# Twelve weight blocks of the second layer's gate moved from TensorE in layer 0 to VectorE in layer 1

## The reference, cut to what matters

```
for l in range(2):
    mod = silu(c) @ w_ada[l] + b_ada[l]              # 2048 -> 6144, one vector
    shift, scale, gate = split(mod, 3)               # 2048 each
    h = rms_norm(x, norm_g[l]) * (1 + scale) + shift
    u, z_s, q, k, v, z_a = split(h @ w_in[l])        # 2048 -> 6144
    y_s = s5_mixer(u, ..., w_glu[l]) * silu(z_s)     # a scan, then 1024 -> 2048
    y_a = diff_attention(q, k, v) * silu(z_a)
    y = concat([y_s, y_a]) @ w_out[l]                # 2048 -> 2048
    x = x + gate * y
```

## Time and profile before

| | us |
|---|---|
| three runs | 2893.7, 2898.98, 2899.66 |
| their median | 2898.98 |
| the profiled execution | 2895.5 |
| its span in the trace | 2893.6 |
| TensorE busy, VectorE busy | 2781.8, 2008.9 |
| layer 0's `w_outa`, `w_glu`, `w_outm` | about 524 to 693 |
| layer 1's `w_outa`, `w_glu`, `w_outm` | 1045.7 to 1185.0 |

### The profile page before, as it was taken

The page is one execution under the profiler, slowest core; times in us unless marked ns, Lnnn a source line. Parts: engine busy times, 40 slices in busy tenths (PEclk is TensorE's granted clock), DMA queues, the critical chain, the costliest instruction groups (busy, mean ns, idle before and its releaser), DMA issues.

```text
span 2893.6 us, 64415 instructions
## 1 busy us (share of the span) xinstructions
PE 2781.8 (96%) x27664; PEld 2593.9 (90%) x27664; DVE 2008.9 (69%) x3478; ACT 1468.2 (51%) x2406; POOL 288.5 (10%) x488
## 2 busy tenths in 40 slices
PE   6899999999999999999999999999999999999987
PEld 2678788788999999999889889999999999999987
DVE  6357778687799986765556566666888547887565
ACT  3335556355566656644444435456555445555454
POOL 0012222100123221200011011100000000000000
PEclk9899999999999999999999999999999999999999
DMA  9988788885756566555444445554555555555543
GB/s 392 332 267 269 260 287 267 292 310 169 205 171 199 175 204 197 181 175 169 140 144 150 140 133 170 180 193 161 185 182 187 184 184 180 181 185 187 182 153 110
DMA packets 168236, 581.08 MB, mean 201 GB/s; under 512 B 40272, under 2 KB 40304, under 8 KB 155536
## 3 DMA queue, kind: packets, MB, share of 16 engines
q1 hardware_dynamic: 146784, 525.40, 54.2%
q0 software_dynamic: 20592, 48.26, 5.4%
q10 hardware_dynamic: 576, 3.31, 0.3%
HBM read 555.06 MB, written 21.76 MB: 199 GB/s over the span
## 4 chain that ended last, share of the span: by engine, by line
PE 84%; DVE 7%; DMA 6%; ACT 1%; issue 1%; SPq 1%; POOL 0%; DVEq 0%; ACTq 0%
PE acc L1011 82%; DMA arena<-in_w_ada 3%; DVE arena L979 2%; PE acc L1014 2%; DVE rounded L979 2%; DMA scr_k<-arena 1%; DMA arena<-scr_k 1%; SPq L976 1%; DVE upper L987 1%; DMA scr_u<-upper 0%; DVE arena L987 0%; ACT arena L1008 0%; DVE rounded L987 0%; DVE upper L979 0%; DMA arena<-in_w_outm 0%
## 5 line engine op out<-in xcount | busy, mean ns | idle before, releaser
L1011 PE MATMUL acc<-rounded 128*128 128x256 f32 x14592 | 1861.9, 286 | 18.6 <-issue 10.1
L1011 PEld LDWEIGHTS acc<-rounded 128*128 128x128 f32 x14592 | 1783.5, 192 | 86.2 <-issue 61.2
L1008 ACT ACTIVATE rounded<-arena 128x1024 fp32r<-128x1024 f32 (+1 forms) x862 | 875.3, 1022 | 694.5 <-PE acc L1011 583.5
L979 DVE TENSOR_TENSOR rounded<-arena,rounded 128x1024 fp32r<-128x1024 f32 (+1 forms) x830 | 983.9, 1198 | 246.7 <-ACT rounded L1008 246.1
L1011 PEld LDWEIGHTS acc<-upper_rounded,rounded 128*128 128x128 f32 x4656 | 560.8, 192 | 18.2 <-issue 9.8
L1011 PE MATMUL acc<-upper_rounded,rounded 128*128 128x256 f32 x4656 | 567.7, 284 | 2.8 <-DVE rounded L979 2.0
L1008 ACT ACTIVATE arena<-arena 128x256 f32<-128x256 f32 (+3 forms) x473 | 232.9, 515 | 170.8 <-DVE arena L979 105.4
L979 DVE TENSOR_TENSOR arena<-acc,arena 128x256 f32<-128x256 f32 (+5 forms) x270 | 113.7, 431 | 233.7 <-PE acc L1011 221.0
L979 DVE TENSOR_TENSOR arena<-arena 128x256 f32<-128x256 f32 (+5 forms) x455 | 233.3, 526 | 35.9 <-ACT arena L1008 27.5
L987 DVE SCALAR_TENSOR_TENSOR arena<-arena 128x256 f32<-128x256 f32 (+5 forms) x465 | 205.1, 446 | 27.7 <-ACT arena L1008 19.6
L1011 PE MATMUL acc<-arena 128*32 128x512 f32 (+6 forms) x1990 | 183.2, 402 | 41.7 <-DMA arena<-in_w_ada 27.6
(11 more groups left out here) (92 smaller groups left out, 1116.0 us busy)
## 6 DMA issues: line engine op xcount, KB each, us to landing
arena<-in_w_in SPq DMA_DIRECT2D x328, 512.0 KB, 4.8
arena<-in_w_ada SPq DMA_DIRECT2D x88, 1024.0 KB, 5.5
arena<-in_w_up SPq DMA_DIRECT2D x176, 512.0 KB, 3.9
arena<-in_w_down SPq DMA_DIRECT2D x88, 512.0 KB, 4.2
arena<-in_w_outa SPq DMA_DIRECT2D x32, 512.0 KB, 6.0
arena<-in_w_glu SPq DMA_DIRECT2D x32, 512.0 KB, 5.8
arena<-in_w_outm SPq DMA_DIRECT2D x32, 512.0 KB, 4.6
arena<-in_w_out SPq DMA_DIRECT2D x32, 512.0 KB, 3.8
```

Of the source, the lines that this page charges most:

```text
L979: return self.put(self.e and self.e.tensor_tensor(o, a, b, op))
L1008: return self.put(self.e and self.e.activation(o, a, f, scale=scale, **kw))
L1011: return self.put(self.e and self.e.matmul(o, l, r, start=start, stop=stop, skip_group_check=True))
```

## The change

- The units of columns 9, 10 and 11 of layer 1 (12 MB of w_ada, the gate of rows 4 to 15) are taken out of layer 0's background. `later` has columns 8 to 11 of layer 0 in one group of four and columns 0 to 8 of layer 1 in groups of three.
- A new generator `g_modv` runs in layer 1 from `w_outa` on. GpSimd loads each unit (`modv_load`, 128x2048, two buffers); the first two loads wait for the scan's last y, each later one for the unit two before it. VectorE multiplies each of a unit's four 128x512 blocks by one value per partition and adds it up (`modv`: one TENSOR_SCALAR for the first block of a column, else SCALAR_TENSOR_TENSOR). At a column's end TensorE sums over the partitions by four matmuls with one column of ones (`modv_end`), and VectorE adds the bias.
- Layer 1's `w_outa` tiles ("xb") are now copied by ScalarE from PSUM into free places of SBUF (`late_tile`). `late_x(n)` adds tile n to x once its gate is known: tiles 0 to 3 after `w_outa`'s tile 3, the others after `modv_end`. An xf tile waits for its late_x.

```diff
 MOD_REST = (2, 3, 2)
+MODV = (9, 10, 11)
+MODV_REST = (6, 1, 1)
...
+        if t.kind == "xb":
+            if n == 7:
+                act.wait_ge("s5_act", ("y", 1, 15))
+            act.act(V(late_tile(n), 256), pv, ACT.Copy).then_inc("ev_act", key)
...
-        later = then(self.modulation(0, range(8, 12), (7,), 2), self.modulation(1, range(12), (7,), 3))
+        later = then(self.modulation(0, range(8, 12), (7,), 4), self.modulation(1, range(MODV[0]), (7,), 3))
+
+        def g_modv():
+            while ("s5", 1, 15) not in self.marks:
+                yield
+            for _ in range(2):
+                yield
+            for u in range(2):
+                self.add("modv_load", u)
+            while ("w_outa", 1, 3) not in self.marks:
+                yield
+            for n in range(4):
+                self.add("late_x", n)
+            for u in range(4 * len(MODV)):
+                for i in range(4):
+                    self.add("modv", u, i)
+                    for _ in range(self.modv_rest):
+                        yield
+                if u + 2 < 4 * len(MODV):
+                    self.add("modv_load", u + 2)
+                if u % 4 == 3:
+                    yield
+                    self.add("modv_end", u // 4)
+                    for n in range(4):
+                        self.add("late_x", 4 * MODV[u // 4] - 32 + n)
+                        yield
...
+    def modv_end(j):
+        pe.wait_ge("modv_dve", (4 * j + 3, 3))
...
+        for i in range(4):
+            x = pe.mm(B(5, i, 1), V(MACC + 512 * (j % 2) + 128 * i, 128), con("ones", 1), True, True)
+        x.then_inc("mod_pe", ("col", (1, MODV[j])))
...
+    def modv(u, i):
+        dve.wait_ge(f"l_mv{u % 2}", u)
...
+            x = dve.ts(acc, w, c, None, MUL)
+        else:
+            dve.wait_ge("modv_dve", (u, i - 1) if i else (u - 1, 3))
+            x = dve.stt(acc, w, c, acc, MUL, ADD)
...
+    def late_x(n):
+        x = V(X + 256 * n, 256)
+        dve.wait_ge("ev_act", ("ev", tl.out_of["w_outa", 1, n].o))
+        dve.wait_ge("mod_dve", ("mod", (1, 8 + n // 4)))
+        dve.stt(x, V(late_tile(n), 256), V(MODC + 80 + n, 1), x, MUL, ADD).then_inc("late_dve", n)
...
+                if t.kind == "xf":
+                    dve.wait_ge("late_dve", n)
...
+    def modv_load(u):
+        if u < 2:
+            pool.wait_ge("s5_act", ("y", 1, 15))
+        else:
+            pool.wait_ge("modv_dve", (u - 2, 3))
+        pool.dma(V(MWS[u % 2], 2048), D["w_ada"][48 + 4 * MODV[0] + u], f"l_mv{u % 2}", u)
```

More of the change, by code:

```diff
@@ L90, in const_array @@
     put("c8", np.broadcast_to(np.arange(32) * 8, (128, 32)))
-    put("quad", p[:, None] % 32 == np.arange(3)[None, :])
+    put("quad", p[:, None] % 32 == np.arange(4)[None, :])
     put("nsgn", np.where(top, -1, 1))
@@ L182, with late_tile @@
 SQF = N1 + 5632 + 6 * 256
+def late_tile(n):
+    return (PQ if n < 4 else APR - 1024 if n < 7 else ACC - 1792) + 256 * n
 def mix_tile(n):
@@ L315, in __init__ @@
         self.o, self.name, self.l, self.n, self.bank, self.before = o, name, l, n, bank, before
-        self.kind = "xf" if (name, l) == ("w_outm", 1) else kind_of(name, n)
+        self.kind = {("w_outm", 1): "xf", ("w_outa", 1): "xb"}.get((name, l)) or kind_of(name, n)
         self.slots = {}
@@ L1975, in modend, with modv_end @@
                ADD).then_inc("mod_dve", *(("mod", (l, j - n)) for n in range(group)))
+    def modv(u, i):
+        dve.wait_ge(f"l_mv{u % 2}", u)
+        w, c = V(MWS[u % 2] + 512 * i, 512), V(CA + 4 * (u % 4) + i, 1)
+        acc = V(MACC + 512 * (u // 4 % 2), 512)
+        if u % 4 == 0 and i == 0:
+            if u >= 8:
+                dve.wait_ge("mod_pe", ("col", (1, MODV[u // 4 - 2])))
+            x = dve.ts(acc, w, c, None, MUL)
+        else:
+            dve.wait_ge("modv_dve", (u, i - 1) if i else (u - 1, 3))
+            x = dve.stt(acc, w, c, acc, MUL, ADD)
+        x.then_inc("modv_dve", (u, i))
+    def modv_end(j):
+        dve.wait_ge("mod_pe", ("col", (1, MODV[j])))
+        at = 48 + 4 * MODV[j]
+        dve.tt(V(MODC + at, 4), B(5, 0, 4), V(PAR + PCOL["b_ada"] + at, 4), ADD).then_inc("mod_dve", ("mod", (1, MODV[j])))
+    def late_x(n):
[3 more added lines that the diff above has]
+        dve.stt(x, V(late_tile(n), 256), V(MODC + 80 + n, 1), x, MUL, ADD).then_inc("late_dve", n)
     def recip(tag):
@@ L2566, in ev @@
                 add_square(t, n == 0, RS2)
-    play = dict(begin=begin, lo=lo, modend=modend, recip=recip, rms2=rms2, lam=lam, tables=tables, gp=gp, h=h, hf=hf, xs=xs, fin=fin, part=part,
+    play = dict(begin=begin, lo=lo, modend=modend, modv=modv, modv_end=modv_end, late_x=late_x, recip=recip, rms2=rms2, lam=lam, tables=tables, gp=gp, h=h, hf=hf, xs=xs, fin=fin, part=part,
                 s5_setup=s5_setup, s5_prep=s5_prep, s5_phase=s5_phase, s5_run=s5_run, s5_out=s5_out, att=att, glu_first=glu_first,
```

27 lines of the change are left out of this document (19 added, 8 removed).

## The result

| | before | after |
|---|---|---|
| median of nine runs, us | 2898.98 | 2910.01 |
| lowest to highest | 2892.66 to 2908.80 | 2903.65 to 2914.30 |
| the profiled execution (its span) | 2895.5 (2893.6) | 2903.69 (2901.9) |

The ratio of the times is 1.0036 (95% interval 1.002 to 1.0051): the change makes the kernel 0.4% slower, 11 us by the medians. The prediction was 2900 with a range of 2887 to 2908, so the time lies 2 us above its top.

The account below looks back on a forecast made before the run. TensorE, busy 96% of the span, was taken as the bound. -17.1 + 2.6 + 5 + 6 + 2 + 2.5 = +1.0 us on the profiled 2895.5 gave 2896.5, put at 2900 for the median; range 2887 to 2908.

Parts of the forecast that it names:

- What leaves TensorE: Layer 0: twelve units, a closing group and some waits go from TensorE, together 17.1 us off.
- what VectorE gives back in layer 0: Layer 0: without the units VectorE loses time to catch up, so TensorE waits for it; 5 us given back.
- full stretch: Layer 0, 604.38 to 643.94 us: VectorE busy 34.4 us where TensorE has 30.2 us left without the units.
- The clock: Layer 1: TensorE's clock falls to half speed behind its wait for the first 1 MB; 2 us more (0 to 3).
- the bound of 8 us: Layer 0: upper bound of the 5 us given back, if three of VectorE's waits stay or TensorE's clock falls.
- The closing groups: Layer 1: three groups of four small matmuls come to TensorE, 0.88 us each, 2.6 us.
- The first load: Layer 1's w_outa: VectorE waits at the first modv for 1 MB, landing at 1068; TensorE waits 6.0 us.
- the fit that it cites: The Trainium skill's GpSimd-issued transfer time, 2.0 us plus bytes over 436 GB/s: 4.4 us for 1 MB, TensorE's wait 1.9.
- w_outm: Layer 1's w_outm: VectorE needs 3.45 us a tile, 0.57 over TensorE's 2.88; TensorE waits 2.5 us (0 to 5).
- B: Rival: first 1 MB holds layer 1; TensorE waits 9 us, clock 3, read back 2, w_outm 5; 2908 us, chance 0.21.
- C: Rival: first 1 MB lands in 5.5 us, TensorE waits 3.0 us, clock need not fall; 2895 us, chance 0.12.
- wait of 1 to 4 us ahead of the third group of 128x1: Sign in layer 1's w_outm: TensorE waits there, VectorE has no idle time from tile 2 to 9.

Follow-up runs that it names:

- e1: Changed kernel without its layer 1 loads of w_ada, modv and modv_end (gate of rows 4 to 15 left out): 2885.76 us, ratio 0.9943 to 0.997.
- e5: Changed kernel without layer 1's sums, but with TensorE's three closing groups put back on constants, not waiting for VectorE: 2889.29 us.
- e2: Changed kernel with the first modv after w_outa's tile 6 instead of 3, one modv every 4 steps instead of 6: 2911.4 us.
- e7: Changed kernel with only columns 10 and 11 summed by VectorE, first modv after w_outa's tile 7: 2905.42 us.
- e8: Changed kernel with only column 11 summed by VectorE, from w_outa's tile 12 on: 2905.11 us.
- e6: Changed kernel with its twelve layer 1 loads of w_ada left out, modv, modv_end and late_x kept: 2902.49 us.
- e3: Changed kernel with GpSimd's sums of squares in layer 1's w_outm cut to one column each: 2904.8 us.
- e16: Changed kernel without layer 1's loads of w_ada and with GpSimd's sums of squares cut to one column each: 2890.65 us.

## Why the prediction was wrong, point by point

**What leaves TensorE and what VectorE gives back in layer 0: right in the sum, in part by luck.** -17.1 + 5 = -12.1 predicted, -13.1 measured by e1. From the last 128x3 group to layer 1's first matmul the profiles have 130.7 against 142.3 us, 11.5 less. The waits came at the end of the full stretch, 4.17 us against 1.04: 3.1 us given back where I had 4.5 to 5. The clock, which I had only in the bound of 8 us, fell behind them, and 4.89 us of work at half clock cost 2.4 more; the two make 5.5. The further 4.3 us up to 520 us in the profile are the change's only for the 0.9 us of one closing group less, which stood at 454 us before: e1, with the same instructions up to there, had 528.1.

**The closing groups: right** (2.5 for 2.6; e5).

**The first load: right in kind, in size by luck.** The place, the wait of VectorE (6.26 us for about 8), the `lo` behind it and the clock at 0.5 are as told. TensorE's wait was 2.9 us in the profile of after and up to 5.2 in the others, not 6.0. In after the first 1 MB landed at 1046.8, 2.5 us sooner than what I took (1068, or 1049.3 in after's time, where layer 1 begins 18.7 us sooner), and TensorE stopped half a us later than I had counted. From issue to landing that 1 MB took 5.9 us and the twelve loads 5.3 to 9.3, where the prediction took 8.4; the 4.4 us of the fit that it cites was too short for every one. With 1.5 us for the half clock the first load cost 4.4 us in after, against the 6 + 2 predicted. But I stopped at that wait: the loads also make y's read back late (e2, e7, e8), and GpSimd's sums pile up behind the late ones. All that they cost is 7.1 us beside the sums of squares (161.5 less e6's 154.4) and 10.5 without them (e3 less e16); that the first of these is near 8 is luck.

**w_outm: the step that failed.** "2.5 us of waiting at that group" stood for what e5 and e6 measure as 12.6 us. The overload by count, which is what I had worked out, is 2.1 of them: a tile takes VectorE 3.25 us alone, where I had 3.45. The other 10.5 are collisions with GpSimd's sums of squares, which I had named in the text ("GpSimd adds the squares") and never set beside VectorE's timeline. I had priced the new operation with 0.66 us, from the 0.69 us of the earlier trace rows, rows of operations that had none of GpSimd's sums beside them. The measured mean in w_glu and w_outm was 995 ns, and the sixteen old 128x256 operations with a rounded result grew too, from 516 to 696 ns. A sign stood in the rows that I cited: a `lo` took 1.23 us in w_glu and 1.33 in w_outm, and the latter began while the second sum of the pair above was still running.

The Trainium skill ("SBUF — State Buffer", section "Who interferes with whom") has the rule: a VectorE instruction with two inputs in SBUF and a GpSimd instruction that reads SBUF exclude each other, and the second to come waits for the first to end. The traces agree that the two do not run at once, with 0.74 turned into 1.23 us for one sum and 3.57 for four. On who goes first they do not: the operation of 3.57 us began 0.18 us ahead of the first sum and still stood for all four. The rule would have led to the rival that was missing.

**The clock: right in kind, counted once instead of four times.** I took 2 us behind the first load. It fell with each wait of 2.88 us or more, three times in layer 1 and once at w_outm's start in layer 0, and 7.9 of the 21.1 us in layer 1 are what work at the lower clock costs. These 7.9 us are part of the 7.1 and 12.6 us above, not an addition to them.

**The rivals.** The direction was that of B, slower by layer 1. Its sizes were not: B has 12 us for the first load and its clock, 2 for the read back and 5 for w_outm; all loads cost 7.1 (10.5 alone), and w_outm 12.6. C had a wait of 3.0 us without a fall of the clock; the wait was 2.88, and the clock fell. The sign that I gave for w_outm was a "wait of 1 to 4 us ahead of the third group of 128x1": that wait was 2.99 us, but two others, 0.97 and 2.90, stood ahead of it, which no step had.

The sum with the measured terms: -13.1 + 2.5 + 7.1 + 12.6 = +9.1 us, against +11.0 by the medians. It is no check of its own: the last three terms are differences between stages that add up to 161.5 - 139.3. What is missing lies in the second block or in the spread of the runs.

## What to carry to other kernels

Before work is moved to an engine, lay the timeline of every engine that shares something with it beside the place, and not only the busy share of the one that takes the work: here VectorE's idle time in a tile was time in which GpSimd worked. A price read from rows where the operation stood alone is a lower bound. And a load that is put into a queue must be priced for what stands behind it in that queue (y's read back, the sums of squares) as well as for the one who waits for its data.

## What the runs showed of the hardware

- A 128x512 SCALAR_TENSOR_TENSOR with both inputs in SBUF took 0.74 us alone, 1.23 with one GpSimd sum to wait for and 3.57 with four in a row; one that reads PSUM and SBUF (128x256, 0.47 us) was not held up. GpSimd's pairs went from 1.43 to 2.42 us at the same time.
- 20 small matmuls that do nothing, near the start, made the kernel before 0.1% faster (0.9979 to 0.9998); the profiles do not say why. 44 in the changed kernel showed no gain (1.0038 against 1.0036). So a difference of 4 us between two programs here need not come from what was meant to be changed.
- The same program's stretch of 520 us up to layer 0's w_outa differed by several us from one profiled execution to the next (520.1 and 527.0 for the changed kernel, 528.1 and 520.2 for the one without sums), so such a stretch tells of a change only where its waits do.
- In the second block, with the same instructions in all programs, TensorE worked between 7.2 and 22.4 us at half clock and was idle for 36.7 to 42.1 us in the eighteen profiles, and its length, 1707.9 to 1717.6 us, followed these two.
